# A two-layer encoder on one core: plain steps moved ahead of the seven short ones, and corrections joined to 1,024 columns

## The chip, the cores and the metric

The kernel runs on one core of one Trainium2 chip. The metric is device time in microseconds (us) of one execution, the median over runs. TensorE (PE in the profile) multiplies, VectorE (DVE) and ScalarE (ACT) prepare operands and take results, GpSimd (POOL) and SyncE (SP) issue the transfers.

## The reference, cut to what matters

```
for layer in range(DEPTH):                      # 2 layers, 256 rows of 2,048 features, float32
    h = rms_norm(x, mixer_norm_w[layer])
    ...                                         # layer 0: windowed attention + gMLP, layer 1: stick-breaking attention
    x = x + mixed                               # mixed = mixer output @ output projection (2,048 x 2,048)
    h = rms_norm(x, ffn_norm_w[layer])
    x = x + swiglu(h, w_ffn_gate[layer], w_ffn_up[layer], w_ffn_down[layer])
def swiglu(h, w_gate, w_up, w_down):            # hidden width 5,632
    return (jax.nn.silu(h @ w_gate) * (h @ w_up)) @ w_down
```

## The kernel before

All 256 rows stay on the chip and the weights stream past them once. A **chunk** is 512 output columns, a **tile** 128 rows of weights. A **unit** of four tiles (1 MB) is one transfer into one of the four slots of `raw`. A **step** works on two tiles: ACT rounds them to a short float (`w_hi`, L717), DVE takes the rest (`w_lo`, L970), and PE multiplies. `w_hi` and `w_lo` have four slots (`RING`), so ACT may start on a step only when PE is done with the step four back.

A **plain** step takes both row halves (tt = 0, 1) of two tiles: 8 matmuls with `w_hi` (L1483, L1484), then 4 with `w_lo` (L1489). Where two chunks a and b share their left side (gate and up, or two output chunks), their first four tiles go by a product scheme with seven instead of eight multiplications: seven **short** steps of 6 matmuls (L1527, L1528, L1531) named `outer` 0, `P`, `Q`, `corner`, `R`, `outer` 2 and `W`. Their weights are partly sums of weights, four of them (P, Q, R, W), made by DVE (L990) into `tsum`; their left sides are sums of rows (`s_hi`, `s_lo`, or `sm_hi`, `sm_lo`). Three partial products lie in PSUM `turn_zb` until DVE turns them into `corr` (`corrections`, L1042 to L1045), which is added when a chunk leaves (`leave`: L1150, L1154) or to the residual (`corrected`, L1061).

The order of all steps is written out by `seven_steps`, and every engine walks that one list. A(k) and B(k) below are the plain steps on tiles k and k+1 of chunk a and b. Before each DVE step whose number is in `sums` stands the weight sum of that name. The orders are "alone" (most pairs), "together", "together" with 12 tiles (the last down projection of each layer) and "opening" (the first gate/up iteration of each layer, directly behind the output projection). The steps of one iteration are numbered from 0.

Side work hangs on step numbers t: ACT and DVE do it behind their step t + 2 (`AHEAD` = 2). For a phase that renews the normalised input (the output projection), that is for each of its four chunks: add the chunk to the residual (`leave`), square it, transpose it in blocks (`fold`), let POOL write it to memory and read it back spread (`bounce`), and `take_at` some steps later split it into `xT_hi` (ACT, L736) and `xT_lo` (DVE, L1120). Chunk c of the residual becomes tiles 4c to 4c+3 of the next phase. For the output projection `take_at` is t = 39 for chunk 2 and t = 45 for chunk 3; its own steps are 0 to 34, so these fall behind steps 6 and 12 of the opening iteration. The root of the norm is taken at t = 37 (`take_root` on ACT, `give_var` on DVE: behind step 4) and refined at t = 38 (`refine`: behind step 5).

PE waits in the first iteration of a phase, for each step of its chunk a, for the `xT_lo` of its tiles (`stationary_ready`, semaphore `fold_lo`).

Of the kernel before, what the change touches and what calls it, by code (L numbers as in the profile page):

```python
# [28 lines left out]
P = 128  # L29
SEQ = 256  # L30
D = 2048
TT = SEQ // P
KT = D // P
CH = 512
# [46 lines left out]
def seven_steps(a, b, tiles, order):  # L81

    A, B = (lambda k: ("plain", a, k)), (lambda k: ("plain", b, k))
    front = [A(4), A(6), ("outer", a, 0), ("P", -1, 0), B(4), ("Q", -1, 0), B(6), ("corner", b, 0), ("R", -1, 0)]
    sums = dict(SUM_AT)
    if order == "opening":
        sums = {2: "P", 4: "Q", 7: "R", 9: "W"}
        steps = (front[:6] + [B(6), ("corner", b, 0), ("R", -1, 0), ("outer", a, 2), ("W", a, 0), A(8), A(10), B(8), B(10), A(12), A(14), B(12), B(14)])
        units = [(a, 4), (b, 0), (a, 0), (b, 4), (a, 8), (b, 8), (a, 12), (b, 12)]
    elif order == "together" and tiles == 12:  # L90
        sums = {2: "P", 4: "Q", 7: "R", 9: "W"}
        steps = front + [("outer", a, 2), ("W", a, 0), A(8), A(10), B(8), B(10)]
        units = [(a, 4), (b, 0), (a, 0), (b, 4), (a, 8), (b, 8)]
    elif order == "together":
        steps = front + [A(8), ("outer", a, 2), ("W", a, 0), A(10), B(8), B(10), A(12), A(14), B(12), B(14)]
        units = [(a, 4), (b, 0), (a, 0), (b, 4), (a, 8), (b, 8), (a, 12), (b, 12)]
    else:
        steps = front + [A(8), ("outer", a, 2), ("W", a, 0)] + [A(k) for k in range(10, tiles, 2)] + [B(k) for k in range(8, tiles, 2)]
        units = [(a, 4), (b, 0), (a, 0), (b, 4)] + [(a, k) for k in range(8, tiles, UNIT)] + [(b, k) for k in range(8, tiles, UNIT)]
    return steps, units, sums  # L100
# [253 lines left out]
def build(nc, x, xT, normw, w_gate, w_up, w_down, w_in, qkw, sinks, gnw, ws, bs, w_out0, w_qkv, w_out1,  # L354
          ident, dist, tri, strict, out):
    es = ExitStack()
    with es:
        def sem(name):
            return es.enter_context(nc.semaphore(name))

        def sb(name, shape, dt=F32, ctx=None):
            return (ctx or es).enter_context(nc.sbuf_tensor(name, shape, dt))
# [10 lines left out]
        x_sb = sb("x_sb", [P, TT, D])  # L373
# [27 lines left out]
        sums = sb("sums", [P, TT * A_PER])  # L401
# [21 lines left out]
        with ExitStack() as c2:  # L423
            hid = sb("hid", [P, TT, CH], F32, c2)
# [4 lines left out]
            corr = sb("corr", [P, 2 * TT, CH], F32, c2)  # L429
# [21 lines left out]
        acc = es.enter_context(nc.psum_tensor("acc", [P, 2, TT, CH], F32))  # L451
# [4 lines left out]
        product = {n: turn_zb[:, q * CH:(q + 1) * CH] for q, n in enumerate((1, 5, 6, 7))}  # L456
# [19 lines left out]
        products_done = sem("products_done")  # L476
        acc_read = sem("acc_read")
# [22 lines left out]
        sum_made, first_taken, corr_made, hid_made = sem("sum_made"), sem("first_taken"), sem("corr_made"), sem("hid_made")  # L500
        s_made, s_rounded, s_split = sem("s_made"), sem("s_rounded"), sem("s_split")
        sm_made, sm_rounded, sm_split, x_corrected = sem("sm_made"), sem("sm_rounded"), sem("sm_split"), sem("x_corrected")
# [446 lines left out]
        def _(dve):  # L949
            links = [0]  # L950

            def link(ins):

                links[0] += 1
                ins.then_inc(dve_chain, 1)
                dve.wait_ge(dve_chain, links[0])
# [82 lines left out]
            def corrections(pair):  # L1039

                dve.wait_ge(first_taken, pair.n + 1)
                link(nc.vector.tensor_tensor(corr[:, 2, :], corr[:, 0, :], product[6], ALU.subtract))  # L1042
                link(nc.vector.tensor_tensor(corr[:, 1, :], product[7], corr[:, 2, :], ALU.add))
                nc.vector.tensor_tensor(corr[:, 2, :], product[5], corr[:, 2, :], ALU.subtract)
                nc.vector.tensor_tensor(corr[:, 3, :], product[5], corr[:, 1, :], ALU.subtract).then_inc(corr_made, 1)  # L1045

            def residual_ready(ph, c):

                if ph.before == 0:
                    dve.wait_ge(x_landed, 16)  # L1050
                else:
                    dve.wait_ge(x_added, 2 * ((ph.before - 1) * (D // CH) + c) + 2)
                    dve.wait_ge(squared, 2 * ph.rows0 * (D // CH))

            def corrected(ph, pair, c):

                residual_ready(ph, c)
                dve.wait_ge(corr_made, pair.n + 1)
                for tt in range(TT):
                    xs = x_sb[:, tt, c * CH:(c + 1) * CH]  # L1060
                    nc.vector.tensor_tensor(xs, xs, corr[:, 2 * (c % 2) + tt, :], ALU.add).then_inc(x_corrected, 1)  # L1061

            def evacuate(it, c, dst, const=None):

                for tt in range(TT):
                    dve.wait_ge(products_done, 2 * it.last_half(c) + tt + 1)
                    if const is None:
                        ins = nc.vector.tensor_scalar(dst[:, tt, :], acc[:, it.pair(c), tt, :], rstd[:, tt:tt + 1], None, ALU.mult)
                    else:
                        ins = nc.vector.tensor_scalar(dst[:, tt, :], acc[:, it.pair(c), tt, :], rstd[:, tt:tt + 1], const,  # L1070
                                                      ALU.mult, ALU.mult)
                    ins.then_inc(acc_read, 1)
# [58 lines left out]
            def leave(it, c):  # L1131

                ph, i = it.ph, it.i
                if ph.name == "in":
                    if c == 1:
                        dve.wait_ge(v_ready, 1)
                    evacuate(it, c, [kv, qs, qs, gs, us, gs, us][c])
                elif ph.name == "qkv":
                    name, g = QKV[i][c]
                    if name == "q":  # L1140
                        evacuate(it, c, qk1, C_DIM ** -0.5)
                    elif name == "k":
                        dve.wait_ge(fold_done, ph.fold(2 * g) + 1)
                        evacuate(it, c, qk1)
                elif it.seven:
                    dve.wait_ge(corr_made, it.pairs[0].n + 1)
                    if c == 0:
                        for tt in range(TT):
                            dve.wait_ge(products_done, 2 * it.last_half(0) + tt + 1)
                            nc.vector.tensor_tensor(hid[:, tt, :], acc[:, it.pair(0), tt, :], corr[:, tt, :], ALU.add).then_inc(acc_read, 1)  # L1150
                        return
                    for tt in range(TT):
                        dve.wait_ge(products_done, 2 * it.last_half(1) + tt + 1)
                        nc.vector.tensor_tensor(corr[:, 2 + tt, :], acc[:, it.pair(1), tt, :], corr[:, 2 + tt, :], ALU.add).then_inc(acc_read, 1)  # L1154
                    dve.wait_ge(silu_done, ph.up0 + i + 1)
                    for tt in range(TT):
                        dve.wait_ge(acc_read, 2 * ph.chunk(i, 1) + tt + 1)
                        nc.vector.scalar_tensor_tensor(out=hid[:, tt, :], in0=corr[:, 2 + tt, :], scalar=rstd[:, tt:tt + 1],
                                                       in1=hid[:, tt, :], op0=ALU.mult, op1=ALU.mult).then_inc(hid_made, 1)
                elif ph.name == "up":  # L1160
                    if c == 0:
                        evacuate(it, c, hid)
                        return
                    dve.wait_ge(silu_done, ph.up0 + i + 1)
                    for tt in range(TT):
                        dve.wait_ge(products_done, 2 * it.last_half(1) + tt + 1)
                        nc.vector.scalar_tensor_tensor(out=hid[:, tt, :], in0=acc[:, it.pair(1), tt, :], scalar=rstd[:, tt:tt + 1],
                                                       in1=hid[:, tt, :], op0=ALU.mult, op1=ALU.mult).then_inc(acc_read, 1)
                else:

                    residual_ready(ph, c)
                    for tt in range(TT):
                        if it.pair_of(c):
                            dve.wait_ge(x_corrected, 4 * BACK_PAIRS.index(it.pair_of(c)) + 2 * (c % 2) + tt + 1)
                        dve.wait_ge(products_done, 2 * it.last_half(c) + tt + 1)
                        xs = x_sb[:, tt, c * CH:(c + 1) * CH]
                        nc.vector.tensor_tensor(xs, acc[:, it.pair(c), tt, :], xs, ALU.add).then_inc(x_added, 1)  # L1177
# [543 lines left out]
```

## Time and profile before

| | |
|---|---|
| median of 3 runs | 2050.72 us (2050.27 to 2052.87) |
| profiled execution | 2051.17 us, its span 2049.4 us |
| PE, DVE, ACT busy | 2033.7, 1661.7, 1087.5 us |
| transfers | 453.72 MB, mean 221 GB/s |
| granted TensorE clock | 1.000 over the span |

The profiled execution's time is its span and 1.8 us around it. A busy PE is one with a matmul in its pipe; matmuls overlap, so a step's length is read from one start to the next. Rows of the timeline give start, duration, engine, line, operation and tiles, and in brackets the idle time ahead of the row with what ended it.

### The profile page before, as it was taken

How to read it: one execution, taken by the hardware profiler on the slowest of the kernel's cores; microseconds unless marked ns; L12 is line 12 of the kernel's file. 1: busy time of each engine (PE TensorE's matmuls, PEld its weight loads, DVE VectorE, ACT ScalarE, POOL GpSimd, SP SyncE). 2: the span in 40 equal slices, each digit the busy share in tenths (PEclk: the TensorE clock that was granted, in tenths of full speed). 3: DMA queues.
4: the chain of work that ended last, by engine and by line, in shares of the span. 5: the costliest groups of instructions: out<-in, count | busy, mean ns of one | idle time of the engine just before them, and what ended most of it. 6: DMA issues, size and time to landing. Idle time of an engine off the chain costs nothing.

```text
span 2049.4 us, 23323 instructions
## 1 busy us (share of the span) xinstructions
PE 2033.7 (99%) x9176; PEld 1675.6 (82%) x9176; DVE 1661.7 (81%) x1859; ACT 1087.5 (53%) x1250; POOL 162.7 (8%) x271
## 2 busy tenths in 40 slices
PE   9999999999999999999999999999999999999999
PEld 8878878888888888888888888878888888888887
DVE  7777898888788887887666777888888788887986
ACT  6565555555445554555555455555554455544453
POOL 1010110010001000011111110110100001000010
PEclk9999999999999999999999999999999999999999
DMA  9665666566665666668767877676566666666664
GB/s 329 216 216 184 219 228 231 200 216 226 207 225 199 216 222 219 211 205 271 248 211 245 266 236 214 219 239 212 205 219 219 220 205 206 232 220 210 208 210 174
DMA packets 216431, 453.72 MB, mean 221 GB/s; under 512 B 10545, under 2 KB 10561, under 8 KB 216065
## 3 DMA queue, kind: packets, MB, share of 16 engines
q1 hardware_dynamic: 197600, 392.72, 56.1%
q0 software_dynamic: 18304, 57.37, 9.3%
q10 hardware_dynamic: 416, 2.13, 0.3%
q8 instruction: 73, 1.20, 0.2%
q14 instruction: 38, 0.30, 0.0%
HBM read 422.82 MB, written 29.36 MB: 221 GB/s over the span
## 4 chain that ended last, share of the span: by engine, by line
PE 60%; issue 29%; DMA 7%; DVE 2%; POOL 2%; ACT 0%; SPq 0%; POOLq 0%; DVEq 0%
PE acc L1483 17%; PE acc L1489 17%; PE acc L1484 17%; DMA spread<-blocks 3%; DMA blocks<-folded 3%; POOL spread L643 2%; PE turn_zb L1531 1%; PE turn_zb L1528 1%; PE turn_zb L1527 1%; PE acc L1531 1%; PE acc L1528 1%; PE acc L1527 1%; DVE w_lo L970 1%; DMA raw<-in_w_in 1%; DVE tsum L990 0%
## 5 line engine op out<-in xcount | busy, mean ns | idle before, releaser
L717 ACT ACTIVATE w_hi<-raw 128x1024 fp32r<-128x1024 f32 x710 | 742.4, 1056 | 494.5 <-PE acc L1489 479.2
L970 DVE TENSOR_TENSOR w_lo<-raw,w_hi 128x1024 fp32r<-128x1024 f32 x710 | 854.2, 1220 | 157.3 <-ACT w_hi L717 154.8
L1483 PE MATMUL acc<-w_hi,xT_hi 128*128 128x512 f32 x1664 | 649.9, 391 | 0.7 <-ACT w_hi L717 0.7
L1484 PE MATMUL acc<-w_hi,xT_lo 128*128 128x512 f32 x1664 | 647.7, 389 | 0.0
L1489 PE MATMUL acc<-w_lo,xT_hi 128*128 128x512 f32 x1664 | 444.9, 389 | 0.0
L1483 PEld LDWEIGHTS acc<-w_hi,xT_hi 128*128 128x128 f32 x1664 | 312.3, 188 | 67.9 <-issue 1.3
L1489 PEld LDWEIGHTS acc<-w_lo,xT_hi 128*128 128x128 f32 x1664 | 312.3, 188 | 65.1
L1484 PEld LDWEIGHTS acc<-w_hi,xT_lo 128*128 128x128 f32 x1664 | 312.4, 188 | 64.7
L717 ACT ACTIVATE w_hi<-tsum 128x1024 fp32r<-128x1024 f32 x136 | 144.5, 1062 | 303.0 <-DVE tsum L990 286.5
L1483 PE MATMUL acc<-w_hi,m_hi 128*128 128x512 f32 x764 | 297.9, 390 | 0.0
L1484 PE MATMUL acc<-w_hi,m_lo 128*128 128x512 f32 x764 | 297.3, 389 | 0.0
L1489 PE MATMUL acc<-w_lo,m_hi 128*128 128x512 f32 x764 | 204.5, 389 | 1.0 <-DVE w_lo L970 1.0
L970 DVE TENSOR_TENSOR w_lo<-tsum,w_hi 128x1024 fp32r<-128x1024 f32 x136 | 165.6, 1218 | 10.3 <-ACT w_hi L717 10.3
L1489 PEld LDWEIGHTS acc<-w_lo,m_hi 128*128 128x128 f32 x764 | 143.2, 188 | 31.5 <-DVE w_lo L970 1.8
L1483 PEld LDWEIGHTS acc<-w_hi,m_hi 128*128 128x128 f32 x764 | 143.4, 188 | 30.2 <-issue 0.2
L1484 PEld LDWEIGHTS acc<-w_hi,m_lo 128*128 128x128 f32 x764 | 143.4, 188 | 29.9
L628 POOL DMA_DIRECT2D blocks<-folded x42 | 30.3, 722 | 1440.7 <-DVE folded L1109 1160.4
L643 POOL DMA_DIRECT2D spread<-blocks x168 | 97.4, 587 | 144.6 <-DMA blocks<-folded 139.5
L990 DVE TENSOR_TENSOR tsum<-tsum,raw 128x1024 f32<-128x1024 f32 x68 | 82.9, 1219 | 0.0
L990 DVE TENSOR_TENSOR tsum<-raw 128x1024 f32<-128x1024 f32 x68 | 82.8, 1218 | 0.0
L1177 DVE TENSOR_TENSOR x_sb<-acc,x_sb 128x512 f32<-128x512 f32 x64 | 41.3, 686 | 47.4 <-PE acc L1489 39.5
L1154 DVE TENSOR_TENSOR corr<-acc,corr 128x512 f32<-128x512 f32 x44 | 28.4, 686 | 59.2 <-PE acc L1489 59.2
(222 smaller groups left out, 1676.8 us busy)
## 6 DMA issues: line engine op xcount, KB each, us to landing
raw<-in_w_gate SPq DMA_DIRECT2D x88, 1024.0 KB, 5.3
raw<-in_w_up SPq DMA_DIRECT2D x88, 1024.0 KB, 5.2
raw<-in_w_down SPq DMA_DIRECT2D x88, 1024.0 KB, 5.3
raw<-in_w_qkv SPq DMA_DIRECT2D x48, 1024.0 KB, 6.7
raw<-in_w_out SPq DMA_DIRECT2D x32, 1024.0 KB, 5.2
raw<-in_w_in SPq DMA_DIRECT2D x26, 1024.0 KB, 6.4
blocks<-folded POOLq DMA_DIRECT2D x42, 512.0 KB, 3.2
spread<-blocks POOLq DMA_DIRECT2D x168, 128.0 KB, 2.9
```

Of the source, the lines that this page charges most:

```text
L628: pool.dma_start(blocks.rearrange("t p n -> p t n"), (p_folded if F < A_KV else folded)[:, :, :]).then_inc(fold_out, 16)
L643: pool.dma_start(back[b * BLK:(b + 1) * BLK].rearrange("j t a r -> j (t a) r"), blocks[:, :, b * P:(b + 1) * P].rearrange("t (a j) r -> j ...
L717: nc.scalar.activation(w_hi[:, h.slot, :, :], source(h), ACTF.Copy).then_inc(hi_ready, 1)
L970: nc.vector.tensor_tensor(w_lo[:, h.slot, :, :], source(h), f32(w_hi[:, h.slot, :, :]), ALU.subtract).then_inc(lo_ready, 1)
L990: nc.vector.tensor_tensor(out_to, a, b, ALU.add).then_inc(sum_made, 1)
L1177: nc.vector.tensor_tensor(xs, acc[:, it.pair(c), tt, :], xs, ALU.add).then_inc(x_added, 1)
L1483: nc.tensor.matmul(dst, hi[:, h.k0 + k, at], wh, start=h.opens and k == 0, stop=False)
L1484: nc.tensor.matmul(dst, lo[:, h.k0 + k, at], wh, start=False, stop=False)
L1489: ins = nc.tensor.matmul(dst, hi[:, h.k0 + k, at], w_lo[:, h.slot, k, :], start=False, stop=h.closes and k == 1)
L1527: nc.tensor.matmul(dst, sh, wh, start=start, stop=False)
L1528: nc.tensor.matmul(dst, sl, wh, start=False, stop=False)
L1531: ins = nc.tensor.matmul(dst, sh, w_lo[:, h.slot, k, :], start=False, stop=stop)
```

## The change

In the "opening" order, the plain steps on tiles 4 to 11 of both chunks now come first (eight of them), then all seven short steps without a plain one between. In the 12-tile order, A(4), A(6), B(4), B(6) come first, then the seven. The units of `raw` and the places of the sums follow. The other orders stay. Apart from the order, DVE's operations on the two row halves are joined where they allow it: the last two of the corrections, the addition of `corr` to the residual, and the addition of `corr` to `acc` when a gate or up chunk leaves. The joined one waits for both row halves.

```
+    short = [("outer", a, 0), ("P", -1, 0), ("Q", -1, 0), ("corner", b, 0), ("R", -1, 0), ("outer", a, 2), ("W", a, 0)]
     if order == "opening":
-        sums = {2: "P", 4: "Q", 7: "R", 9: "W"}
-        steps = (front[:6] + [B(6), ("corner", b, 0), ("R", -1, 0), ("outer", a, 2), ("W", a, 0), A(8), A(10), B(8), B(10), A(12), A(14), B(12), B(14)])
-        units = [(a, 4), (b, 0), (a, 0), (b, 4), (a, 8), (b, 8), (a, 12), (b, 12)]
+        sums = {8: "P", 9: "Q", 11: "R", 13: "W"}
+        steps = [A(4), A(6), B(4), B(6), A(8), A(10), B(8), B(10)] + short + [A(12), A(14), B(12), B(14)]
+        units = [(a, 4), (b, 4), (a, 8), (b, 8), (a, 0), (b, 0), (a, 12), (b, 12)]
     elif order == "together" and tiles == 12:
-        sums = {2: "P", 4: "Q", 7: "R", 9: "W"}
-        steps = front + [("outer", a, 2), ("W", a, 0), A(8), A(10), B(8), B(10)]
-        units = [(a, 4), (b, 0), (a, 0), (b, 4), (a, 8), (b, 8)]
+        sums = {4: "P", 5: "Q", 7: "R", 9: "W"}
+        steps = [A(4), A(6), B(4), B(6)] + short + [A(8), A(10), B(8), B(10)]
+        units = [(a, 4), (b, 4), (a, 0), (b, 0), (a, 8), (b, 8)]
...
-                nc.vector.tensor_tensor(corr[:, 2, :], product[5], corr[:, 2, :], ALU.subtract)
-                nc.vector.tensor_tensor(corr[:, 3, :], product[5], corr[:, 1, :], ALU.subtract).then_inc(corr_made, 1)
+                nc.vector.tensor_tensor(corr[:, 2:4, :], product[5].unsqueeze(1).to_broadcast([P, TT, CH]), corr[:, 2:0:-1, :],
+                                        ALU.subtract).then_inc(corr_made, 1)
...
-                for tt in range(TT):
-                    xs = x_sb[:, tt, c * CH:(c + 1) * CH]
-                    nc.vector.tensor_tensor(xs, xs, corr[:, 2 * (c % 2) + tt, :], ALU.add).then_inc(x_corrected, 1)
+                xs = x_sb[:, :, c * CH:(c + 1) * CH]
+                nc.vector.tensor_tensor(xs, xs, corr[:, 2 * (c % 2):2 * (c % 2) + TT, :], ALU.add).then_inc(x_corrected, TT)
...
-                    for tt in range(TT):
-                        dve.wait_ge(products_done, 2 * it.last_half(1) + tt + 1)
-                        nc.vector.tensor_tensor(corr[:, 2 + tt, :], acc[:, it.pair(1), tt, :], corr[:, 2 + tt, :], ALU.add).then_inc(acc_read, 1)
+                    dve.wait_ge(products_done, 2 * it.last_half(1) + TT)
+                    nc.vector.tensor_tensor(corr[:, TT:, :], acc[:, it.pair(1), :, :], corr[:, TT:, :], ALU.add).then_inc(acc_read, TT)
```

DVE at the first opening iteration, from its work on step 2 of that iteration on (`L1177` adds the output projection's chunk 3, `xT_lo` is chunk 2's take). Before:

```order
208 L1177 TENSOR_TENSOR x_sb<-acc,x_sb 128x512 x2
209 L990 TENSOR_TENSOR tsum<-raw 128x1024
210 L970 TENSOR_TENSOR w_lo<-raw,w_hi 128x1024
211 L1109 STREAM_TRANSPOSE folded<-x_sb 128x512 x2
212 L970 TENSOR_TENSOR w_lo<-tsum,w_hi 128x1024
213 L990 TENSOR_TENSOR tsum<-raw 128x1024
214 L970 TENSOR_TENSOR w_lo<-raw,w_hi 128x1024
215 L1082 TENSOR_REDUCE var<-squares 128x2
...
217 L970 TENSOR_TENSOR w_lo<-tsum,w_hi 128x1024
...
222 L970 TENSOR_TENSOR w_lo<-raw,w_hi 128x1024
223 L1120 SCALAR_TENSOR_TENSOR xT_lo<-spread,normw_sb,xT_hi 128x256 x4
```

The same place in the changed kernel:

```order
207 L1175 TENSOR_TENSOR x_sb<-acc,x_sb 128x512 x2
208 L971 TENSOR_TENSOR w_lo<-raw,w_hi 128x1024
209 L1109 STREAM_TRANSPOSE folded<-x_sb 128x512 x2
210 L971 TENSOR_TENSOR w_lo<-raw,w_hi 128x1024 x2
211 L1082 TENSOR_REDUCE var<-squares 128x2
...
213 L971 TENSOR_TENSOR w_lo<-raw,w_hi 128x1024
...
218 L971 TENSOR_TENSOR w_lo<-raw,w_hi 128x1024
219 L1120 SCALAR_TENSOR_TENSOR xT_lo<-spread,normw_sb,xT_hi 128x256 x4
```

The two sums (L990) are gone from this stretch; the take of chunk 2 keeps its place behind the seventh step's `w_lo`. What was `w_lo` of P and of Q is now `w_lo` of plain steps.

PE at the fifth step of that iteration (number 4), the end of the step ahead of it and its first rows, with the semaphores that a row waits for. Before, B(4):

```order
951 L1531 MATMUL turn_zb<-w_lo,s_hi 128x512 [waits lo_ready]
952 L1531 MATMUL turn_zb<-w_lo,s_hi 128x512
953 L1483 MATMUL acc<-w_hi,xT_hi 128x512 [waits x_added,hi_ready]
954 L1484 MATMUL acc<-w_hi,xT_lo 128x512
955 L1483 MATMUL acc<-w_hi,xT_hi 128x512
956 L1484 MATMUL acc<-w_hi,xT_lo 128x512
```

In the changed kernel, A(8):

```order
969 L1487 MATMUL acc<-w_lo,xT_hi 128x512 [waits lo_ready]
970 L1487 MATMUL acc<-w_lo,xT_hi 128x512 x3
971 L1481 MATMUL acc<-w_hi,xT_hi 128x512 [waits hi_ready,fold_lo]
972 L1482 MATMUL acc<-w_hi,xT_lo 128x512
973 L1481 MATMUL acc<-w_hi,xT_hi 128x512
974 L1482 MATMUL acc<-w_hi,xT_lo 128x512
```

A(8) was step 11 and is now step 4; with it moves PE's wait for `fold_lo`, here for the take of chunk 2.

## Rows read from the trace of the kernel before

**Rows 1.** The page's busy line (us, share of span, instructions), and the clock by core.

```profile
PE 2033.7 (99%) x9176; PEld 1675.6 (82%) x9176; DVE 1661.7 (81%) x1859; ACT 1087.5 (53%) x1250; POOL 162.7 (8%) x271
...
core 0: 2049.4 us, clock 1.000
```

**Rows 2.** Timeline of TensorE, first opening iteration (step 0 starts at 267.05).

```profile
267.05 0.39 PE L1483 MATMUL acc<-w_hi,xT_hi 128*128 128x512 f32 x1
...
269.77 0.39 PE L1483 MATMUL acc<-w_hi,xT_hi 128*128 128x512 f32 x1
...
274.70 0.50 PE L1531 MATMUL turn_zb<-w_lo,xT_hi 128*128 128x512 f32 x1 [1.15 <-DVE w_lo L970]
...
288.03 0.73 PE L1531 MATMUL acc<-w_lo,s_hi 128*128 128x512 f32 x2 [1.38 <-DVE w_lo L970]
288.60 0.40 PE L1527 MATMUL turn_zb<-w_hi,s_hi 128*128 128x512 f32 x1
...
290.01 0.40 PE L1527 MATMUL turn_zb<-w_hi,xT_hi 128*128 128x512 f32 x1
```

**Rows 3.** Windows: length, PE busy (records), clock, DMA share, GB/s; both opening iterations.

```profile
267.05:304.36 37.31, 33.15 (x140) 1.00 0.62 205
1339.70:1377.10 37.40, 33.26 (x140) 1.00 0.62 204
```

**Rows 4.** Timeline of TensorE, layer 0's 12-tile pair, step 13.

```profile
934.21 0.39 PE L1483 MATMUL acc<-w_hi,m_hi 128*128 128x512 f32 x1
...
936.68 1.19 PE L1489 MATMUL acc<-w_lo,m_hi 128*128 128x512 f32 x4 [0.49 <-DVE w_lo L970]
```

**Rows 5.** Timeline of VectorE, first opening iteration.

```profile
271.10 1.28 DVE L1177 TENSOR_TENSOR x_sb<-acc,x_sb 128x512 f32<-128x512 f32 x2
...
279.35 0.17 DVE L1083 TENSOR_SCALAR var<-var 128x2 f32<-128x2 f32 x1
...
284.04 1.67 DVE L1120 SCALAR_TENSOR_TENSOR xT_lo<-spread,normw_sb,xT_hi 128x256 fp32r<-128x256 f32 x4
```

**Rows 6.** Timeline of ScalarE, first opening iteration.

```profile
275.57 1.28 ACT L686 ACT_TABLE_LOAD   x1
279.55 0.20 ACT L744 ACTIVATE log<-var 128x2 f32<-128x2 f32 x1 [2.69 <-DVE var L1083]
...
281.79 1.69 ACT L736 ACTIVATE xT_hi<-spread,normw_sb 128x256 fp32r<-128x256 f32 x4
283.39 1.05 ACT L717 ACTIVATE w_hi<-raw 128x1024 fp32r<-128x1024 f32 x1
```

**Rows 7.** Timeline of GpSimd: chunk 2's way back.

```profile
266.14 2.32 POOL L643 DMA_DIRECT2D spread<-blocks  x4 [3.47 <-DMA blocks<-folded]
```

**Rows 8.** Timeline of VectorE, 12-tile pair, layer 0.

```profile
933.00 2.50 DVE L1061 TENSOR_TENSOR x_sb<-x_sb,corr 128x512 f32<-128x512 f32 x4
935.41 2.35 DVE L970 TENSOR_TENSOR w_lo<-raw,w_hi 128x1024 fp32r<-128x1024 f32 x2
```

**Rows 9.** Timeline of VectorE and TensorE between two ordinary gate/up iterations.

```profile
357.40 1.29 DVE L1154 TENSOR_TENSOR corr<-acc,corr 128x512 f32<-128x512 f32 x2 [2.74 <-PE acc L1489]
358.61 1.40 DVE L1158 SCALAR_TENSOR_TENSOR hid<-corr,rstd,hid 128x512 f32<-128x512 f32 x2
...
363.42 1.18 DVE L970 TENSOR_TENSOR w_lo<-tsum,w_hi 128x1024 fp32r<-128x1024 f32 x1
...
365.33 0.62 PE L1531 MATMUL turn_zb<-w_lo,s_hi 128*128 128x512 f32 x2
```

**Rows 10.** Groups of VectorE by form: busy us, mean ns, idle before.

```profile
L1154 DVE TENSOR_TENSOR corr<-acc,corr 128x512 f32<-128x512 f32 x44 | 28.4, 686 | 59.2 <-PE acc L1489 59.2
L1100 DVE TENSOR_TENSOR m_lo<-turn_zb,m_hi 128x1024 fp32r<-128x1024 f32 x6 | 7.3, 1223 | 3.7 <-ACT m_hi L724 3.7
```

**Rows 11.** Timeline of TensorE: matmuls of 128 columns at the kernel's start and later.

```profile
1.00 5.90 PE L1661 MATMUL turn_zb<-ones_sb 128*128 128x128 f32 x28 [1.00 <-POOL ones_sb L615]
...
148.60 2.05 PE L1584 MATMUL turn_zb<-gs,wsT 128*128 128x128 f32 x16 [1.23 <-DVE gs L1268]
```

More of the change, by code:

```diff
@@ L1147, in leave @@
                     if c == 0:
-                        for tt in range(TT):
-                            dve.wait_ge(products_done, 2 * it.last_half(0) + tt + 1)
-                            nc.vector.tensor_tensor(hid[:, tt, :], acc[:, it.pair(0), tt, :], corr[:, tt, :], ALU.add).then_inc(acc_read, 1)
+                        dve.wait_ge(products_done, 2 * it.last_half(0) + TT)
+                        nc.vector.tensor_tensor(hid[:, :, :], acc[:, it.pair(0), :, :], corr[:, 0:TT, :], ALU.add).then_inc(acc_read, TT)
                         return
-                    for tt in range(TT):
-                        dve.wait_ge(products_done, 2 * it.last_half(1) + tt + 1)
-                        nc.vector.tensor_tensor(corr[:, 2 + tt, :], acc[:, it.pair(1), tt, :], corr[:, 2 + tt, :], ALU.add).then_inc(acc_read, 1)
+                    dve.wait_ge(products_done, 2 * it.last_half(1) + TT)
+                    nc.vector.tensor_tensor(corr[:, TT:, :], acc[:, it.pair(1), :, :], corr[:, TT:, :], ALU.add).then_inc(acc_read, TT)
                     dve.wait_ge(silu_done, ph.up0 + i + 1)
```

## The prediction

> **What bounds the kernel now.** I read the page first: TensorE is busy for 2033.7 of 2049.4 us at a clock of 1.000 [rows 1]. A busy engine can still be late, so next I read its timeline for rows that begin later than the spacing of their neighbours. A plain step is 12 matmuls and takes 2.72 us from start to start (267.05 to 269.77), 0.227 us each; a short one takes 1.4 us (288.60 to 290.01) [rows 2]. Against these lengths, what is lost stands in few places. The largest two are the opening iterations. The window from step 0 to the start of A(12) is 37.31 us [rows 3]; it holds eight plain and seven short steps, 8 x 2.72 + 7 x 1.4 = 31.5 us. So 5.8 us are lost, and 5.8 again in layer 1, whose window is as long to 0.1 us. The brackets of the late rows name `w_lo` as what was waited for (two of them are shown) [rows 2]. The 12-tile pair loses 0.65 us in step 13: its `w_lo` matmuls begin at 936.68, where 934.21 + 8 x 0.227 = 936.03 was due [rows 4]. With layer 1's, which looks the same, there are some 13 us in all that this change could touch.
>
> **The change part by part.**
>
> *Opening, the front.* By the list of steps, PE would now do A(4), A(6), B(4), B(6) without a weight sum and reach A(8) at 267.05 + 4 x 2.72 = 277.93. Is B(4) in time? DVE adds chunk 3 from 271.10 to 272.38 [rows 5], which PE needs for B(4)'s accumulator at 267.05 + 2 x 2.72 = 272.49; the sum P that followed is gone, so B(4)'s `w_lo` follows at once, 272.3 to 273.5, and is due at 272.49 + 1.81 = 274.30. In time, and B(6)'s after it too.
>
> A(8), though, is a step of chunk a, and PE waits ahead of it for chunk 2's `xT_lo`. The take of chunk 2 is tied to the step count and not to its data: the data was sent for by 268.5 [rows 7], and the take still began on ACT at 281.79 [rows 6] and ended on DVE at 284.04 + 1.67 = 285.71 [rows 5]. In the changed order it stands behind the same seventh step, and DVE's program ahead of it is the one of before without the sums P and Q. A 1,024-wide operation that follows another holds DVE for 2.35 - 1.22 = 1.14 us [rows 8]; two make 2.28. The joined corrections of the output projection, a little upstream on a DVE that is then never idle, give 0.25 (one and two joins at 2 x 0.61 - 1.14 = 0.08, with 0.61 = (2.50 - 0.68) / 3 [rows 8]). So the take ends at 285.71 - 2.53 = 283.2. ACT keeps pace: its table load would begin some 0.6 us earlier and be over before `var`, at 279.35 + 0.17 - 2.5 = 277.0; the logarithm, the root, two `w_hi` and the take of before follow at the same distances [rows 6]. PE waits from 277.9 to 283.2: **5.3 us lost where there was at most 1.4 in one place.** What is late next is nothing for a while, since A(8) to B(10) have their `w_lo` ready.
>
> *Opening, the seven in a row.* `outer` 0 starts at 283.2 + 4 x 2.72 = 294.1. The sum P and later Q were made during the plain steps. Seven short steps are 9.8 us of PE, against 7 x 1.14 of `w_lo` and two or three sums, so what PE hid before is now tight: ACT rounds R when `outer` 0 is done (295.5 + 0.2 + 1.06 = 296.8), then takes chunk 3 (1.6 us [rows 6], to 298.4; its data is long back), DVE the low part (1.6, to 300.0), the sum W (301.2) and the `w_lo` of `outer` 2, 302.4. That is due at 294.1 + 5 x 1.4 + 0.93 = 302.0, so 0.4 us are lost. A(12) starts at 267.05 + 31.5 + 5.3 + 0.4 = 304.3, where it started at 304.36. **The term is -0.1 us per opening.** Behind it the corrections come later, beside four plain steps (10.9 us) in which DVE has four `w_lo` and 2.8 us of corrections: hidden; without that cover they would cost 2.7. The raw units are requested no later in the front than before.
>
> *12-tile pairs.* DVE works without a pause from the evacuation at the pair's start to the end of step 13's `w_lo`, 935.41 + 1.22 = 936.63 [rows 8]. The set of its operations there stays, so the order does not help: PE reaches step 13 with the same steps behind it. What moves is the start, by the joined `corr<-acc` (0.5 us later, next part), less one join of the corrections and two of `corrected`, 3 x 0.08. `w_lo` ends 0.2 us later, and the loss grows from 0.65 to 0.85: **+0.2 us per pair**, twice. A(8)'s take ends some 0.3 us ahead of A(8), so nothing there.
>
> A page bears on the joins. By the Trainium skill, page "VectorE: DVE Perf Modes", section "The TRN2 errata — SBUF-src ops pay a fixed extra latency per instruction", a float32 tensor_tensor takes (N + 151) cycles at 0.96 GHz, 691 ns for 512 and 1,224 for 1,024; the trace agrees (686 and 1,223 [rows 10]). By the page's duration a join saves 0.16 us, and the pair's term would be about 0; I go by the rows' starts, 0.08, since operations overlap at their ends.
>
> *Joined evacuations.* Between two iterations DVE started `corr<-acc` at 357.40, when the first row half was done, 0.45 us (two matmuls) before the second. Joined, it starts at 357.85, takes 1.22 (a 1,024-wide read of PSUM takes 1,223 ns [rows 10]), and `hid` must wait for all of it: 359.1 in place of 358.61 [rows 9], 0.5 us later. Queued behind it are the sum P, two `w_lo`, the transposes and P's `w_lo`, which ended at 363.42 + 1.18 = 364.60 and was due at 365.33. Of 0.73 us of slack 0.2 stay. There are 20 such boundaries, all at nothing. The price if the shift is longer: 20 x (shift - 0.73). The joins of gate chunks meet more slack.
>
> **Sum**: 2 x (-0.1) + 2 x 0.2 + 0 = +0.2 us on the profiled 2051.17, so 2051.4; the median of the runs lies 0.45 below the profiled one, which gives 2050.9, said as **2051.0 us**. Each opening's wait may be off by 0.7 either way (ACT's start of the root, the landing of semaphores), so its own range is 2049.3 to 2053.
>
> **The rivals.**
>
> *A: the clock falls in the new wait* (slower). No idle of TensorE inside the span exceeds 1.4 us, and the clock never fell; an idle of 5.3 us is new. At the kernel's start, after standing idle, the same 128-column matmul ran 28 records in 5.90 us, 0.21 each, where later 16 took 2.05, 0.13 each [rows 11]: the start is at 1.2 GHz and not at 2.4, though the window views count it as 1.00. Such a spell costs 28 x 0.083 = 2.3 us. That is my upper bound for one fall, and nothing the lower one. One fall gives 2053.3, both openings 2055.6. It decides for "slower" only if both fall at the full price. For it: the idle is nearly four times the longest of before. Against: nothing in this trace.
> The Trainium skill, page "TensorE: Matmul & The Clock Gate", section "Part 1: The HAM clock gate", says that the clock halves after an idle stretch and comes back only with sustained work, which speaks against this change: by it one fall or two are more likely than none.
>
> *B: A(8) does not wait* (faster). If the take were done early, the 5.3 us would go, and each opening would lose the short run's 0.4 alone: 2051.0 - 10.6 = 2040.4. For it: chunk 2's data is back ten us before the take. Against it: the order of DVE shows the take behind seven `w_lo`, and PE's row of A(8) waits for `fold_lo`.
>
> *C: the joined evacuation uses up the slack* (slower). At a shift of 1.0 us, 20 x 0.27 = 5.4: 2056.4. It reaches +4 us from a shift of 0.93, that is, if the joined operation takes 0.43 longer than 1.22. Against: the PSUM row of that width.
>
> **How the numbers follow.** No fall, as summed: 0.47. One fall or two cheap ones: 0.29. Both at full price: 0.12. B, or a wait much shorter than 5.3: 0.08. C: 0.04. A measurement tells about 0.2%, 4.1 us, from no change; so faster 0.08, same 0.77, slower 0.15. The range must take in the falls, up to 2055.6, and waits a little shorter: 2048 to 2056; what is left out is B and part of C.
>
> **What would show it.** In the profile after: the window from step 0 to A(12) again 37 to 38 us long, in one idle of 5 us ahead of A(8), ended by `xT_lo` (L1120), in place of five small ones behind `w_lo`; that take ending 2.5 us earlier; a short wait at `outer` 2; step 13 of the 12-tile pairs late by 0.8; P's `w_lo` some 0.2 ahead of need at the boundaries; the granted clock under 1.00 in the ten us after A(8) if A holds. I am wrong if A(8) starts near 278, or if ordinary iterations have become longer.

## The result, and the profile after

| | before | after |
|---|---|---|
| median of 7 runs each, on one chip | 2051.51 us (2050.27 to 2053.0) | 2058.48 us (2056.57 to 2061.96) |
| profiled execution, its span | 2051.17, 2049.4 us | 2059.31, 2057.4 us |

The ratio is 1.0035 (95% interval 1.0023 to 1.0047): slower by 7 us, outside the predicted range. The page of after, its busy line and its clock line:

```profile
PE 2036.8 (99%) x9176; PEld 1676.9 (82%) x9176; DVE 1657.3 (81%) x1757; ACT 1085.6 (53%) x1250; POOL 162.7 (8%) x271
...
core 0: 2057.4 us, clock 0.998
```

VectorE has 102 instructions and 4.4 us less to do, and the span is 8 us longer: what it did less was not what set the end. And the clock reads 0.998 where it was 1.000 [rows 1]. It was 0.997 or 0.998 in each of the seven runs.

The view of waits of TensorE in after gives the total, the count and the longest for each pair of line and releaser:

```profile
PE acc L1481 <- DVE xT_lo L1120: 10.4, 2, 5.2
PE acc L1487 <- DVE w_lo L971: 1.8, 2, 0.9
```

Two waits of 5.2 us stand where the openings had several small ones. The two of 0.9 are step 13 of the 12-tile pairs. Now the timeline of TensorE in after: the first opening at A(8) and at `outer` 2, then the second at A(8).

```profile
282.76 0.79 PE L1481 MATMUL acc<-w_hi,xT_hi 128*128 128x512 f32 x1 [5.22 <-DVE xT_lo L1120]
283.35 0.63 PE L1482 MATMUL acc<-w_hi,xT_lo 128*128 128x512 f32 x1
283.78 0.63 PE L1481 MATMUL acc<-w_hi,xT_hi 128*128 128x512 f32 x1
...
286.21 1.08 PE L1487 MATMUL acc<-w_lo,xT_hi 128*128 128x512 f32 x4
287.14 0.39 PE L1481 MATMUL acc<-w_hi,xT_hi 128*128 128x512 f32 x1
287.37 0.40 PE L1482 MATMUL acc<-w_hi,xT_lo 128*128 128x512 f32 x1
...
303.63 0.50 PE L1529 MATMUL turn_zb<-w_lo,xT_hi 128*128 128x512 f32 x1 [0.24 <-DVE w_lo L971]
...
1360.32 0.80 PE L1481 MATMUL acc<-w_hi,xT_hi 128*128 128x512 f32 x1 [5.23 <-DVE xT_lo L1120]
```

The wait is not the whole loss. Step 0 began at 266.50, so A(8) was due at 266.50 + 4 x 2.72 = 277.38 and began 5.38 us late. Then it took 287.14 - 282.76 = 4.38 us, though every operand was there: 1.66 more than a plain step's 2.72. Behind the wait the spacing is 0.43 us (283.35 to 283.78), at the next step 0.23 again (287.14 to 287.37). In the second opening A(8) began 5.39 us late and took 4.86, 2.14 too much. The windows of after say why. The columns are those of [rows 3]: length, TensorE's busy time (records), clock, DMA share, GB/s.

```profile
266.50:305.61 39.11, 33.65 (x140) 0.96 0.55 158
277.00:282.70 5.70, 0.54 (x3) 0.99 0.99 284
282.70:286.00 3.30, 3.24 (x8) 0.50 1.05 279
286.00:290.00 4.00, 4.00 (x19) 0.99 0.93 295
1344.05:1383.60 39.55, 34.08 (x139) 0.91 0.52 156
```

From the start of step 0 to that of A(12) the two openings are 1.80 and 2.26 us longer than before (these windows cut off up to 0.05 us of the second). In the first, the clock still reads 0.99 over the idle and 0.50, the level of 1.2 GHz, in the 3.3 us after it. In the second it fell while TensorE still waited. The windows there, with the columns of all engines (busy time and records of TensorE, its weight loads, VectorE, ScalarE and GpSimd, then clock, DMA share, GB/s):

```profile
1355.10:1357.80 2.70, 0.00 (x0) 0.00 (x0) 2.13 (x6) 2.70 (x6) 1.76 (x4) 1.00 1.03 338
1357.80:1360.30 2.50, 0.00 (x0) 0.00 (x0) 2.50 (x6) 1.19 (x2) 0.55 (x1) 0.51 1.01 270
1360.30:1364.70 4.40, 4.38 (x10) 3.51 (x11) 2.24 (x2) 0.00 (x0) 0.00 (x0) 0.50 1.05 290
```

What set the wait is the take, here on VectorE in after:

```profile
276.35 0.17 DVE L1083 TENSOR_SCALAR var<-var 128x2 f32<-128x2 f32 x1
...
281.04 1.67 DVE L1120 SCALAR_TENSOR_TENSOR xT_lo<-spread,normw_sb,xT_hi 128x256 fp32r<-128x256 f32 x4
```

It ended at 282.71, 16.2 us behind step 0, where before it was 285.71 - 267.05 = 18.7 [rows 5]: 2.5 us earlier. But A(8) now needed it at 277.38.

The boundary that answers to [rows 9], VectorE and TensorE in after (this iteration starts on TensorE at 358.97; before, it started at 357.59):

```profile
359.27 1.23 DVE L1152 TENSOR_TENSOR corr<-acc,corr 128x1024 f32<-128x1024 f32 x1 [3.22 <-PE acc L1487]
360.60 1.42 DVE L1156 SCALAR_TENSOR_TENSOR hid<-corr,rstd,hid 128x512 f32<-128x512 f32 x2
...
365.43 1.18 DVE L971 TENSOR_TENSOR w_lo<-tsum,w_hi 128x1024 fp32r<-128x1024 f32 x1
...
366.71 0.69 PE L1529 MATMUL turn_zb<-w_lo,s_hi 128*128 128x512 f32 x2
```

P's `w_lo` ended at 366.61, 0.10 us before TensorE took it at 366.71. Before, 0.73 us lay between. The pair of matmuls lasts 0.69 where it had 0.62.

Last, step 13 of the 12-tile pair, which answers to [rows 4] and [rows 8], on TensorE and VectorE in after:

```profile
936.34 0.39 PE L1481 MATMUL acc<-w_hi,m_hi 128*128 128x512 f32 x1
...
939.18 1.20 PE L1487 MATMUL acc<-w_lo,m_hi 128*128 128x512 f32 x4 [0.87 <-DVE w_lo L971]
```

```profile
935.63 2.36 DVE L1061 TENSOR_TENSOR x_sb<-x_sb,corr 128x1024 f32<-128x1024 f32 x2
937.91 2.36 DVE L971 TENSOR_TENSOR w_lo<-raw,w_hi 128x1024 fp32r<-128x1024 f32 x2
```

It is late by 939.18 - (936.34 + 8 x 0.227) = 1.02 us, after 0.65.

### The profile page after: what moved, and what is told of

Same layout as the page of the kernel before. It is cut to its first block, busy times and chain, and to the rows that moved or that the text cites. A ratio compares the mean times of both kernels' runs of the same rounds, so it can differ in the third digit from the quotient of the medians.

```text
span 2057.4 us, 23243 instructions
## 1 busy us (share of the span) xinstructions
PE 2036.8 (99%) x9176; PEld 1676.9 (82%) x9176; DVE 1657.3 (81%) x1757; ACT 1085.6 (53%) x1250; POOL 162.7 (8%) x271
## 4 chain that ended last, share of the span: by engine, by line
PE 86%; DVE 7%; issue 3%; DMA 2%; ACT 1%; POOL 0%; DVEq 0%; POOLq 0%; ACTq 0%
PE acc L1481 23%; PE acc L1487 23%; PE acc L1482 23%; DVE w_lo L971 3%; PE turn_zb L1529 3%; PE turn_zb L1526 3%; PE turn_zb L1525 3%; PE acc L1529 2%; PE acc L1526 2%; PE acc L1525 2%; DMA blocks<-folded 1%; DVE tsum L991 1%; DMA spread<-blocks 1%; DMA w_blocks<-w_folded 1%; DVE folded L1109 0%
## 5 line engine op out<-in xcount | busy, mean ns | idle before, releaser
L1152 DVE TENSOR_TENSOR corr<-acc,corr 128x1024 f32<-128x1024 f32 x22 | 26.9, 1225 | 67.3 <-PE acc L1487 67.3
```

## Where the time went, stretch by stretch

The starts of the steps on TensorE's timeline cut each profile into stretches. This table, worked out from them, gives each stretch's difference to before in us; the kernels are explained below.

```
                               before    after  opening  twelve   joins  filled  early  order+early  best   evac   half
two opening iterations          96.39    +4.07   +5.86   -0.03   -0.41   +0.48  -9.50     -9.14     -9.46  -0.03  +0.56
other gate/up/down iterations 1185.89    +1.91   -0.01    0.00   +2.27   +2.32  +2.36     +0.01      0.00  +1.96  +2.32
12-tile pairs' phases          127.09    +0.84    0.00   -0.02   +0.89   +0.86  +0.87     +0.02     -1.58  +1.23  +0.84
qkv, in, out                             +1.32   +3.8    +1.1    +0.4    +0.5   -0.6      +1.8      +3.5   -1.3   -1.0
```

Three parts change with the edits: +4.07, +1.91 and +0.84 are 6.8 us, against 7.0 between the medians. The last row does not follow the edits: "opening" and "half" have the same order of work there, and their differences are +3.8 and -1.0. In it single waits for late transfers come and go from one profile to the next, such as this of ScalarE in after, in the qkv phase of layer 1:

```profile
1111.38 1.06 ACT L903 ACTIVATE kT_hi<-spread 128x1024 fp32r<-128x1024 f32 x1 [4.26 <-DMA spread<-blocks]
```

That row is, as I read it, scatter of single profiles, -1.3 to +3.8 us; the medians are over many runs. But the +3.8 of "opening" holds a third fall of the clock. At the same step of the qkv phase where before has 0.41 us of idle, TensorE in "opening" stood for 2.36 us, and the step behind it took 996.66 - 992.21 = 4.45 us in place of 2.72. TensorE's timeline, and the window behind the idle:

```profile
992.21 0.60 PE L1484 MATMUL acc<-w_hi,xT_hi 128*128 128x512 f32 x1 [2.36 <-ACT w_hi L718]
...
996.66 0.39 PE L1484 MATMUL acc<-w_hi,xT_hi 128*128 128x512 f32 x1
```

```profile
992.20:995.90 3.70, 3.69 (x9) 2.91 (x10) 3.56 (x7) 2.80 (x3) 1.77 (x4) 0.54 0.66 178
```

## The experiments

My theory after the result: the clock's fall in the new wait costs the openings' part, and the joined evacuations cost the rest. The rivals: the openings are longer for another reason, say the seven short steps in a row or transfers, and the ordinary iterations for the joined corrections or by scatter.

### One part of the change alone

**Opening order alone** ("opening"), on the kernel before:

```
-        steps = (front[:6] + [B(6), ("corner", b, 0), ("R", -1, 0), ("outer", a, 2), ("W", a, 0), A(8), A(10), B(8), B(10), A(12), ...
+        sums = {8: "P", 9: "Q", 11: "R", 13: "W"}
+        steps = [A(4), A(6), B(4), B(6), A(8), A(10), B(8), B(10)] + short + [A(12), A(14), B(12), B(14)]
+        units = [(a, 4), (b, 4), (a, 8), (b, 8), (a, 0), (b, 0), (a, 12), (b, 12)]
```

> The kernel before with the new opening order alone. Theory 1 (the wait ahead of A(8) lets the clock fall): the changed kernel's windows from step 0 to A(12) were 39.1 us against 37.3 and some 2.2 us longer in layer 1, so this kernel takes +3.5 to +5 us, ratio 1.0017 to 1.0024, with an idle of 5.4 us ahead of A(8) and a granted clock of 0.50 behind it. Theory 2 (the joins cost most of it): +1 us or less. Theory 3 (later transfers do): about +7, as the whole change.

Measured: 2056.84 us (median of 12, 2055.48 to 2060.76), ratio 1.0022 (1.0014 to 1.003). The clock was 0.996 to 0.998 in every run. A(8) waited 5.39 and 5.41 us and then took 2.56 and 2.37 us more than 2.72. In the first opening the clock stayed at 0.50 longer, and the step behind A(8) took 0.37 too much as well, so that this fall cost 2.9 us. The windows of this kernel behind the first wait, with all engines:

```profile
283.00:287.00 4.00, 3.71 (x9) 2.97 (x10) 2.51 (x3) 0.00 (x0) 0.00 (x0) 0.50 1.06 265
287.00:289.50 2.50, 2.50 (x8) 1.98 (x7) 0.00 (x0) 0.62 (x1) 0.00 (x0) 0.53 1.03 351
```

So the opening order carries more than half of the loss, and with it the fall; the ordinary iterations are as before (-0.01).

**12-tile order alone** ("twelve"): `sums`, `steps` and `units` of the 12-tile branch as in the change, nothing else.

```
+        sums = {4: "P", 5: "Q", 7: "R", 9: "W"}
+        steps = [A(4), A(6), B(4), B(6)] + short + [A(8), A(10), B(8), B(10)]
+        units = [(a, 4), (b, 4), (a, 0), (b, 0), (a, 8), (b, 8)]
```

> The kernel before with the new order of the 12-tile pairs alone. Theory 1: the set of VectorE's operations ahead of step 13 is the same and it never pauses there, so step 13 is late by 0.6 to 0.7 us as before and the time is the same, -0.3 to +0.3 us. Rival: the seven short steps in a row cost VectorE or TensorE a wait of their own, +1 us or more for the two pairs.

Measured: 2051.24 us (11 runs), ratio 0.9994 (0.9985 to 1.0002); step 13 late by 0.63 and 0.64 as before. The order does nothing, since the same VectorE work stands ahead of step 13 in both.

**All joins alone** ("joins"): the three edits of VectorE's operations, no order changed.

```
+                nc.vector.tensor_tensor(corr[:, 2:4, :], product[5].unsqueeze(1).to_broadcast([P, TT, CH]), corr[:, 2:0:-1, :],
+                xs = x_sb[:, :, c * CH:(c + 1) * CH]
+                    dve.wait_ge(products_done, 2 * it.last_half(1) + TT)
```

> The kernel before with the joined operations alone. Theory 1: the ordinary iterations of the changed kernel were 0.05 to 0.12 us longer each, and the 12-tile pairs' step 13 later by 0.4, so +1.5 to +2.5 us in all. Theory 2 (the joins cost most): +5 or more. Rival (the joins are free, the iterations' growth is chance of one profile): 0 or less.

Measured: 2054.51 us (11 runs), ratio 1.0008 (1.0 to 1.0017). The interval touches 1. The profile tells more, with ordinary iterations +2.27 and 12-tile phases +0.89, as in after.

**Joined evacuations alone** ("evac"), to part them from the joined corrections:

```
-                    for tt in range(TT):
-                        dve.wait_ge(products_done, 2 * it.last_half(1) + tt + 1)
-                        nc.vector.tensor_tensor(corr[:, 2 + tt, :], acc[:, it.pair(1), tt, :], corr[:, 2 + tt, :], ALU.add).then_inc(acc_read, 1)
+                    dve.wait_ge(products_done, 2 * it.last_half(1) + TT)
+                    nc.vector.tensor_tensor(corr[:, TT:, :], acc[:, it.pair(1), :, :], corr[:, TT:, :], ALU.add).then_inc(acc_read, TT)
```

> The kernel before with the joined evacuations alone (the two additions of corr to acc). Theory 1: it carries all that the joins cost in ordinary iterations, +0.1 us in each of twenty, 2.3 us, and makes the 12-tile pairs' step 13 later by 0.5, since nothing is given back: +2.5 to +3.5 us. Rival (the joined corrections cost): +1 us or less.

Measured: 2053.48 us (11 runs), ratio 1.0009 (1.0 to 1.0018). That is +1.9 us, where +2.5 to +3.5 were expected. In the profile the ordinary iterations have +1.96 and the 12-tile phases +1.23, more than with all joins, 3.2 together. Step 13 on TensorE in this kernel:

```profile
934.60 0.39 PE L1481 MATMUL acc<-w_hi,m_hi 128*128 128x512 f32 x1
...
937.59 1.19 PE L1487 MATMUL acc<-w_lo,m_hi 128*128 128x512 f32 x4 [1.01 <-DVE w_lo L970]
```

It is 1.17 us late, against 0.65 before, 1.02 in after and 0.95 in "joins". So the evacuation join costs 0.5 per pair and the joined corrections give 0.15 to 0.2 back. Scatter falls as a rival: the six profiles with joined evacuations have +1.9 to +2.4 in the ordinary iterations, those without 0.0. That the joined corrections cost something falls only for themselves: "best" has them without the joined evacuations, and its ordinary iterations have 0.00. Beside joined evacuations one thing stays open. One iteration of layer 1 is 0.4 to 0.5 us longer in all five profiles with every join, and 0.11 in "evac". Its `hid` began late, here on VectorE in after:

```profile
1438.89 1.42 DVE L1156 SCALAR_TENSOR_TENSOR hid<-corr,rstd,hid 128x512 f32<-128x512 f32 x2 [0.46 <-DVE corr L1152]
```

In "evac" and in "best" this row has no idle ahead of it.

### The wait and the clock

**The wait filled** ("filled"): after, and TensorE runs 18 matmuls of ones, whose results nothing uses, ahead of A(8). The wait itself stays.

```
+                if it.ph.name == "up" and it.ph.part == 0 and it.i == 0 and h.s == 4:
+                    pe.wait_ge(corr_made, h.pair.n)
+                    for _ in range(18):
+                        nc.tensor.matmul(turn[:, 0:P], ones_sb[:, :], ones_sb[:, :], start=True, stop=True)
```

> The changed kernel with 18 matmuls of ones (128 columns, into a PSUM bank that is free there) put in front of A(8) of both opening iterations, so that TensorE works through most of the wait of 5.4 us. They add nothing that is used. Theory 1: the wait for the low part stays (A(8) starts at the same place), but the clock stays at 1.00 behind it, A(8) takes 2.7 us and not 4.4, and the time falls by 3 to 4.5 us against the changed kernel, to about 2054 to 2055. Rival (the clock column does not tell TensorE's pace, the long A(8) has another cause): A(8) stays 4.4 us long, no change against 2058.

Measured: 2056.52 us (12 runs), ratio 1.002 (1.0011 to 1.0028), clock 1.000 in nine runs and 0.999 in three. By the medians beside before, 2 us of the 7 are gone, less than the expected 3 to 4.5, and the interval overlaps that of after. The profiles part the two kernels. TensorE's timeline in this kernel (each of the 18 matmuls leaves two records):

```profile
277.57 4.18 PE L1458 MATMUL turn_zb<-ones_sb 128*128 128x128 f32 x36
282.97 0.50 PE L1485 MATMUL acc<-w_hi,xT_hi 128*128 128x512 f32 x1 [1.23 <-DVE xT_lo L1120]
283.31 0.39 PE L1486 MATMUL acc<-w_hi,xT_lo 128*128 128x512 f32 x1
...
285.83 0.39 PE L1485 MATMUL acc<-w_hi,xT_hi 128*128 128x512 f32 x1
```

A(8) begins 16.28 us behind step 0, as in after (16.26), but takes 2.86 us in place of 4.38. The openings are +0.48, not +4.07: 3.6 us were the clock's. This is the run that shows the cause, since the wait for the take, the order and the transfers are those of after and only the idle is filled. The rival of another reason falls.

**A shorter wait** ("half"): after, with chunk 2's take one step number earlier (t = 38). I wanted to see whether an idle of 3.3 us keeps the clock.

```
+        if self.ph.name == "out" and c == 2:
+            return self.fold_at(c) + 7
```

> The changed kernel with the take of chunk 2 one step number earlier (t = 38, behind step 5), so that the wait ahead of A(8) is about 3.3 us in place of 5.4, where runs so far had either 1.5 us and less or 5.4. Theory 1 with the clock falling only after an idle about as long as the one of the changed kernel: the clock stays at 1.00 in all or most runs, the openings are 2 x (2.1 + 1.7 to 2.2) shorter than in the changed kernel, about 2050 to 2051. Rival (an idle of 3.3 us is enough): the clock falls too, about 2053 to 2055.

Measured: 2054.82 us (10 runs), ratio 1.0016 (1.0007 to 1.0026). The wait came out at 3.9 us, and the clock fell in all ten runs (0.997 to 0.998). The row of A(8) and the windows of this kernel behind it, with all engines:

```profile
281.55 0.80 PE L1483 MATMUL acc<-w_hi,xT_hi 128*128 128x512 f32 x1 [3.75 <-DVE xT_lo L1122]
```

```profile
282.00:284.00 2.00, 2.00 (x6) 1.54 (x6) 1.97 (x3) 0.00 (x0) 0.00 (x0) 0.50 1.01 282
284.00:286.00 2.00, 2.00 (x9) 1.62 (x8) 1.69 (x2) 0.00 (x0) 0.00 (x0) 0.83 1.11 269
286.00:288.00 2.00, 2.00 (x11) 1.65 (x10) 0.81 (x1) 1.06 (x1) 0.00 (x0) 1.00 1.00 267
```

I had expected the clock to stay. A(8) took 4.29 and 4.14 us, 1.6 and 1.4 too much, and in the second opening the step behind it 0.3 more: the fall costs nearly as much behind 3.9 us of idle as behind 5.4. Between 1.54 us, the longest idle up to which no profile has a fall, and the 3.75 us of this row there are two more idles on record. Behind the 2.36 us of "opening" the clock fell. Behind 2.53 us in the qkv phase of layer 1 in "best" it did not, as that kernel's TensorE row and window show:

```profile
1180.52 0.39 PE L1559 MATMUL turn_zb<-kT_hi,qT_hi 128*128 128x256 f32 x1 [2.53 <-DVE kT_lo L1361]
```

```profile
1180.50:1184.00 3.50, 3.48 (x25) 3.31 (x26) 3.50 (x5) 2.34 (x3) 0.72 (x1) 1.00 0.23 81
```

So an idle of 2.4 us can be enough, one of 2.5 need not be, and what decides between them stays open.

### The wait taken away

**Both takes early** ("early"): after, with chunk 2 taken at t = 36 and chunk 3 at t = 42, three steps earlier each.

```
+        if self.ph.name == "out" and c == 2:
+            return self.fold_at(c) + 5
+        if self.ph.name == "out" and c == 3:
+            return self.fold_at(c) + 7
```

> The changed kernel with the take of the output projection's chunk 2 three step numbers earlier (t = 36, behind step 3 of the opening iteration) and of chunk 3 three earlier (t = 42, behind step 9). Theory 1: chunk 2's low part is then ready at about 277, A(8) starts at 278 without a wait or with one under 0.5 us, the clock stays at 1.00, and the opening windows shrink from 39.1 to 32 us or little more: -13 us against the changed kernel, about 2045. Rival (the seven short steps in a row need the head start that the wait gave): the wait moves into the short steps, 1 to 3 us per opening, and the time is 2047 to 2051.

Measured: 2044.02 us (5 runs, 2043.38 to 2046.25; before 2051.54 beside it), ratio 0.996 (0.9948 to 0.9973), clock 1.0. VectorE's take, then TensorE's A(8) and the step behind it:

```profile
275.42 1.67 DVE L1124 SCALAR_TENSOR_TENSOR xT_lo<-spread,normw_sb,xT_hi 128x256 fp32r<-128x256 f32 x4
```

```profile
277.72 0.39 PE L1485 MATMUL acc<-w_hi,xT_hi 128*128 128x512 f32 x1
...
280.44 0.39 PE L1485 MATMUL acc<-w_hi,xT_hi 128*128 128x512 f32 x1
```

Step 0 began at 266.84: A(8) comes 10.88 behind it, 4 x 2.72, without a wait. The take's data was there by 275.42; only the step number had held it back. The openings are 9.50 us shorter than before, by the small waits that the new order removes. The ordinary iterations still have their +2.36.

**Order and early takes, no joins, old 12-tile order** ("order+early"), on the kernel before: the diff of "opening" and that of "early".

> The kernel before with the new opening order and the two earlier takes, no joins and the old 12-tile order. Theory 1: the openings lose next to nothing, so 5.8 us less each than before: 2040 to 2042. It differs from the kernel before it in the job by the joins' 3 us and the 12-tile order's nothing. Rival (the short steps starve): 2044 to 2048.

Measured: 2043.08 us (5 runs), ratio 0.9955 (0.9941 to 0.9968), a little above the expected 2040 to 2042. The openings have -9.14, the ordinary iterations and 12-tile pairs 0.0: the -8.5 us between the medians (-9.2 by the ratio) is the openings'.

**With the joins that help** ("best"): "order+early", and the corrections and the residual's corrections joined, but not the evacuations. In 12-tile pairs the second chunk's residual correction comes a step later:

```
-                        if t == pair.summed + (c % 2 if it.ph.tiles == KT else 0):
+                        if t == pair.summed + c % 2:
```

> The kernel with new opening order and earlier takes, and besides the joined corrections and joined residual corrections but not the joined evacuations; in the 12-tile pairs chunk b's residual correction comes one step later. Theory 1 (of the joins only the evacuation costs): ordinary iterations are as long as in the kernel before, step 13 of the 12-tile pairs is not late any more, 0.65 us less in each: 2039 to 2041. Rival (every join costs): ordinary iterations 0.05 to 0.1 us longer, 2041 to 2044.

Measured: 2040.81 us (5 runs, 2039.29 to 2043.6), ratio 0.9944 (0.9931 to 0.9957). VectorE ahead of step 13 in this kernel, and then TensorE at step 13:

```profile
927.44 1.23 DVE L1065 TENSOR_TENSOR x_sb<-x_sb,corr 128x1024 f32<-128x1024 f32 x1
928.58 1.22 DVE L975 TENSOR_TENSOR w_lo<-raw,w_hi 128x1024 fp32r<-128x1024 f32 x1
929.72 1.22 DVE L1065 TENSOR_TENSOR x_sb<-x_sb,corr 128x1024 f32<-128x1024 f32 x1
```

```profile
928.73 0.39 PE L1487 MATMUL acc<-w_hi,m_hi 128*128 128x512 f32 x1
...
930.54 0.84 PE L1493 MATMUL acc<-w_lo,m_hi 128*128 128x512 f32 x3
```

`w_lo` now stands between the two corrections, ends at 929.80, and is taken at 930.54 = 928.73 + 1.81, on time; the 12-tile phases are 1.58 us shorter. Openings -9.46, ordinary iterations 0.00. It is some 11 us faster than before and 18 us faster than the changed kernel.

## Why the prediction was wrong, point by point

**Right: the wait.** A(8) was to wait 5.3 us for chunk 2's `xT_lo`, on a take ending 2.5 us earlier; it waited 5.38, and the take ended 2.5 earlier. The wait at `outer` 2, 0.4 by the prediction, is 0.4 to 0.5: `outer` 0 to A(12) took 305.61 - 295.32 = 10.29 us for 9.8 of work. With the clock held, the openings were +0.48 in all and the prediction's term -0.2. Rival B did not hold in after. The early takes made its condition true, and gave -9.5 where it had worked out -10.6.

**Right: what a joined operation takes.** It was put at 1,223 ns. Groups of VectorE in after, columns as in [rows 10]:

```profile
L1045 DVE TENSOR_TENSOR corr<-turn_zb,corr 128x1024 f32<-128x1024 f32 x34 | 41.6, 1224 | 1.2
...
L1152 DVE TENSOR_TENSOR corr<-acc,corr 128x1024 f32<-128x1024 f32 x22 | 26.9, 1225 | 67.3 <-PE acc L1487 67.3
```

**Wrong: that no fall of the clock was the likeliest.** This is the step that failed: the prediction's sum put the clock behind the new wait at nothing. Rival A held in both openings of the profile, and the mean clock was under 1.000 in all seven runs. The prediction wrote "Against: nothing in this trace" and still gave 0.47 to no fall. Its bound of 2.3 us for one fall [rows 11] fits after (1.7 and 2.2, and 3.6 for both by the filled wait against after), but not "opening", where the two cost 2.9 and 2.4. The trace had one instance, TensorE at 1.2 GHz after standing idle. The Trainium skill, page "TensorE: Matmul & The Clock Gate", section "Part 1: The HAM clock gate", says that the clock halves after an idle stretch. The runs agree, at 3.9 and at 5.4 us of idle. With the two falls at their measured price the sum would have been 2055.

**Wrong in size: the joined evacuations, "all at nothing".** A start 0.5 us later against 0.73 of slack. The delay was 0.6: the joined operation started 0.30 us behind the iteration's start and not 0.26, `hid` 360.60 - 358.97 = 1.63 behind it where it stood 358.61 - 357.59 = 1.02 behind [rows 9], and P's `w_lo` kept 0.1 us, not 0.2. And this 0.1 was not enough: in after a boundary cost 0.05 to 0.12 us, one of them 0.49 (the late `hid` above), and together 1.9 us over 20. In the terms of the prediction, rival C's formula 20 x (shift - 0.73) gives nothing at 0.6. Its threshold was wrong, since it counted slack as used up only at zero. That the matmul pair's 0.69 in place of 0.62 comes from weights loaded late is my reading of the row, not tested.

**Wrong in size: the 12-tile pairs**, +0.2 each. The delay grew from 0.65 to 1.02, +0.4 each. That the order would not help was right ("twelve"), and so was the direction of both joins. The evacuation join is worth 0.5 ("evac"), as predicted. The joined corrections give 0.15 to 0.2 back where the prediction had 3 x 0.08 = 0.24, and it rounded the rest of 0.26 down to 0.2.

**Together**: 4.1 for the openings, 1.9 and 0.8, against the predicted -0.2, 0 and +0.4. Of the 6.6 us between the sums the clock is 3.6, the boundaries 1.9, the openings with the clock held 0.7 and the 12-tile pairs 0.4.

## What to carry to other kernels

When a change gathers many small stalls of TensorE into one long one, charge the long one twice: its own length, and the slow clock of the matmuls behind it, 1.6 to 2.9 us here. Before moving steps past a piece of side work that is tied to a step number, look when its data arrives and move the side work along: here that turned +4 us into -9.5. Joining two operations is worth doing where the inputs of both are ready together, as in the corrections. Where the two halves become ready one after the other, the join gives up the early start, and here a slack of 0.1 us was not enough to hide that.

## What the runs showed of the hardware

- An idle of TensorE ahead of A(8), 3.75 us by the profile's rows, was enough for the clock to fall in both openings of the profile of "half", and the mean clock was 0.997 or 0.998 in all ten runs. One idle of 2.36 us was followed by a fall, one of 2.53 us was not, and none up to 1.54 us was in any profile here.
- The clock seems to fall now and then in the kernel before too: in five of its 35 runs beside "opening" the mean clock was 0.998 or 0.999, and these took 2054 to 2058 us against the median of 2051.8. None of these runs has a profile, so where it fell stays open.
- The price of a fall varied: 1.6 and 1.8 us in "half", 1.7 and 2.2 in after, 2.9 and 2.4 in "opening", 1.7 for its third fall.
- At 1.2 GHz a 512-column matmul followed the next by 0.43 us, at 2.4 GHz by 0.227: 1.9 times, not quite 2.
- 18 matmuls of 128 columns that compute nothing of use, 4.2 us of TensorE, kept the clock at 1.00 through the wait, though 1.2 us of idle stayed behind them.
